# w_out of a hybrid SSD and attention layer as three products of split float32 parts, with a new order around it

## What is computed

```
for i in range(DEPTH):                       # DEPTH = 2
    x = x + 0.5 * swiglu(rms_norm(x, ffn1_norm[i]), ...)
    h = rms_norm(x, mix_norm[i])
    proj = h @ w_in[i]
    z, xbc, dt_raw, q, k, v = jnp.split(proj, splits, axis=-1)
    xbc = jax.nn.silu(causal_depthwise_conv(xbc, conv_w[i], conv_b[i]))
    y_ssd = ssd_mixer(xbc, dt_raw, z, ...)   # ends with y*silu(z) and a norm per group
    ...
    y_att = dilated_attention(q, k, v).reshape(b, s, ATT_WIDTH)
    x = x + jnp.concatenate([y_ssd, y_att], axis=-1) @ w_out[i]
    x = x + 0.5 * swiglu(rms_norm(x, ffn2_norm[i]), ...)
```

## Time and profile before

| | us |
|---|---|
| median of three runs | 2320.53 |
| lowest and highest of them | 2316.15, 2330.11 |
| the profiled execution's own time | 2322.31 |
| its span in the profile | 2320.5 |
| mean granted clock of PE over the span | 0.974 of full |

### The profile page before, as it was taken

One profiled execution on the slowest core, in us unless ns is written; L12 is line 12 of the kernel. 1 busy time (PEld: TensorE's weight loads), 2 busy tenths in 40 slices (PEclk: granted clock), 3 DMA queues, 4 the chain that ended last, 5 costly groups with the idle time before them and its releaser, 6 DMA issues.

```text
span 2320.5 us, 33951 instructions
## 1 busy us (share of the span) xinstructions
PE 2173.7 (94%) x12936; PEld 1850.1 (80%) x12936; DVE 1617.4 (70%) x2310; ACT 1058.2 (46%) x1267; POOL 446.3 (19%) x235
## 2 busy tenths in 40 slices
PE   5999999999999999899999989999889999999995
PEld 5998999569998998898579988988566777767774
DVE  5755869348558655878367553681389999999997
ACT  3333153334334341343234322212068888887874
POOL 8501644017007104372035000000000000000000
PEclk9999999999999999999999999999989999999998
DMA  8664655246656664464156643345458888888883
GB/s 247 223 194 146 208 156 190 73 136 227 208 174 209 207 198 159 153 201 141 55 200 200 207 145 109 111 126 198 164 198 335 345 341 342 342 339 332 335 343 130
DMA packets 241023, 484.25 MB, mean 209 GB/s; under 512 B 12660, under 2 KB 180880, under 8 KB 224560
## 3 DMA queue, kind: packets, MB, share of 16 engines
q1 hardware_dynamic: 226880, 443.58, 55.2%
q0 software_dynamic: 11424, 37.44, 4.8%
q10 hardware_dynamic: 2640, 2.14, 0.3%
HBM read 482.03 MB, written 1.09 MB: 208 GB/s over the span
## 4 chain that ended last, share of the span: by engine, by line
PE 70%; DVE 18%; ACT 7%; issue 3%; DMA 1%; DVEq 0%; ACTq 0%
PE misc L708 9%; PE misc L709 9%; PE misc L710 9%; PE misc L820 8%; DVE ring_low L2600 6%; PE acc L978 4%; PE acc L708 3%; ACT high_b L1754 3%; PE acc L710 3%; PE acc L709 3%; PE misc L1229 3%; PE misc L1231 2%; DVE arena L2097 2%; DVE ring_low L1981 2%; PE misc L1217 1%
## 5 line engine op out<-in xcount | busy, mean ns | idle before, releaser
L708 PE MATMUL misc<-xl,high_b 128*128 128x256 f32 x1408 | 395.8, 281 | 15.2 <-DVE ring_low L1981 15.2
L709 PE MATMUL misc<-xh,ring_low 128*128 128x256 f32 x1408 | 394.2, 280 | 0.0
L710 PE MATMUL misc<-xh,high_b 128*128 128x256 f32 x1408 | 393.9, 280 | 0.0
L2600 DVE TENSOR_TENSOR ring_low<-ring,high_b 128x2048 fp32r<-128x2048 f32 x128 | 287.0, 2284 | 6.8 <-ACT high_b L1754 6.8
L708 PEld LDWEIGHTS misc<-xl,high_b 128*128 128x128 f32 x1408 | 267.9, 190 | 19.6 <-issue 13.8
L709 PEld LDWEIGHTS misc<-xh,ring_low 128*128 128x128 f32 x1408 | 268.0, 190 | 3.3
L710 PEld LDWEIGHTS misc<-xh,high_b 128*128 128x128 f32 x1408 | 268.9, 191 | 0.0
L820 PE MATMUL misc<-xnT,ring 128*128 128x256 f32 x1152 | 253.2, 381 | 0.0
L820 PEld LDWEIGHTS misc<-xnT,ring 128*128 128x128 f32 x1152 | 219.1, 191 | 30.4 <-issue 0.8
L1981 DVE TENSOR_TENSOR ring_low<-ring,high_b 128x2048 fp32r<-128x2048 f32 x88 | 221.2, 2555 | 23.9 <-ACT high_b L1517 23.9
L1548 ACT ACTIVATE arena<-arena 128x256 f32<-128x256 f32 x88 | 36.8, 418 | 434.2 <-DVE arena L2015 434.2
(11 more groups left out here) (375 smaller groups left out, 4472.9 us busy)
## 6 DMA issues: line engine op xcount, KB each, us to landing
ring<-in_w_dram SPq DMA_DIRECT2D x128, 1024.0 KB, 7.0
ring<-in_w_in_dram SPq DMA_DIRECT2D x72, 1024.0 KB, 5.7
ring_d<-in_w_dram SPq DMA_DIRECT2D x128, 512.0 KB, 5.3
ring<-in_ffn_w_gate_dram SPq DMA_DIRECT2D x44, 1024.0 KB, 5.5
ring<-in_ffn_w_up_dram SPq DMA_DIRECT2D x44, 1024.0 KB, 7.9
ring_d<-in_ffn_w_down_dram SPq DMA_DIRECT2D x88, 512.0 KB, 7.5
arena<-in_w_ada_dram POOLq DMA_DIRECT2D x48, 512.0 KB, 5.0
ring<-in_w_out_dram SPq DMA_DIRECT2D x20, 1024.0 KB, 5.0
```

The costliest lines, as they stand in the source:

```text
L708: pe.matmul(dst, wh, ml, start=start, stop=False, **kw)
L709: pe.matmul(dst, wl, mh, start=False, stop=False, **kw)
L710: return pe.matmul(dst, wh, mh, start=False, stop=stop, **kw)
L2600: dve.tensor_tensor(ring_low[:, s, :], ring[:, s, :], high_b[:, s, :].bitcast(F32), ALU.subtract)\
```

## The change

- `out_rows` uses `three`: twelve fp32r matmuls in place of four float32 ones. ACT makes the high part of each of w_out's eight 1 MB blocks (`high_out`), DVE the low part (`low_out`). The high parts lie in three homes (`OUT_HOME`), each reused when its block has been read. The turned outputs are split too: ACT writes the high part (`y_high`), DVE the low part (`y_low`).
- The SSD's squares move from DVE to ACT (an ACTIVATE with Square behind `high_out(0)` and `high_out(1)`); DVE makes the first low part instead, and waits for the squares.
- Each group of `yt` and each turned group of heads is now drained by ACT and then DVE, not by one of them.
- `TURNS` comes one step later, `UNITS` has another order, and row 13 stands behind the last turn.
- SP waits for blocks 6 and 7 of w_out to be read before it loads the first rows of `w_down` of the second feed-forward layer.

```diff
-TURNS = {7: 0, 11: 1, 15: 2}
-UNITS = {0: 0, 1: 1, 2: 2, 3: 3, 4: 4, 7: 5, 8: 8, 9: 9, 11: 6, 12: 10, 13: 11, 15: 7, 16: 12, 18: 13}
+TURNS = {8: 0, 12: 1, 16: 2}
+UNITS = {0: 0, 1: 1, 2: 2, 3: 3, 4: 4, 6: 5, 9: 8, 10: 9, 11: 6, 12: 7, 13: 10, 15: 11, 17: 12}
+OUT_HOME = {0: 0, 1: 1, 2: 2, 3: 1, 4: 0, 5: 2, 6: 0, 7: 1}
+OUT_HIGHS = {1: 2, 5: 4, 7: 3, 9: 5, 12: 6, 15: 7}
+OUT_LOWS = {0: 1, 2: 2, 6: 4, 8: 3, 10: 5, 14: 6, 16: 7}
...
                     for q in range(2):
                         load_pair(n, i, q, w[0], w[1], c * P + q * BLK)
+                        if which and not q:
+                            for b in (6, 7):
+                                wait_slot_read(sp, RING["wout", l] + b)
                         for j in range(2 * q, 2 * q + 2):
...
                 def out_rows(k, halves=range(2)):
-                    n = n0 + k // 2
-                    if k >= KD:
-                        wait_drained(pe, m0 + AF["Y", (k - KD) // 2])
-                    wait_slot(n)
-                    w = rows_part(n)
+                    b = k // 2
+                    n = n0 + b
+                    wait_drained(pe, m0 + AF["Y", (k - KD) // 2] if k >= KD else FILL["yt", l] + k // 2)
+                    wait_split(pe, low_in, n)
+                    wh, wl = out_high_rows(b)[:, k % 2, :], out_low_rows(n)[:, k % 2, :]
...
-                            mm = pe.matmul(acc[:, t, c * 512:(c + 1) * 512], yT[:, k, t * P:(t + 1) * P],
-                                           w[:, k % 2, c * 512:(c + 1) * 512], start=(k == 0), stop=(k == 15),
-                                           skip_group_check=True)
+                            ts = slice(t * P, (t + 1) * P)
+                            mm = three(acc[:, t, cs], y_high(k)[:, ts], y_low(k)[:, ts], wh[:, cs], wl[:, cs],
+                                       k == 0, k == 15, skip_group_check=True)
...
                 turn_values(3)
+                out_rows(13).then_inc(freed[(n0 + 6) % SLOTS], 1)
                 out_rows(14, [0])
...
+            def high_out(l, b):
...
+                act.wait_ge(loaded[n % SLOTS], LOAD * (n // SLOTS + 1))
+                act.activation(out_high(b), ring[:, n % SLOTS, :], ACT.Copy).then_inc(high_in[n % SLOTS], 1)
...
+                for b in range(2):
+                    high_out(l, b)
+                act.wait_ge(yz_ready, l + 1)
+                act.activation(xdt.rearrange("p t e -> p (t e)"), xtok.rearrange("p t e -> p (t e)"), ACT.Square)\
+                    .then_inc(ysq_ready, 1)
                 act.wait_ge(sq_ready, 2 * l + 2)
                 act.activation(gss, gs, ACT.Sqrt).then_inc(std_ready2, 1)
...
+                for q in range(4):
+                    ssd_turned(q)
                 for h in range(HEADS + 2):
...
                     if h in TURNS:
                         values_turned(TURNS[h])
+                    if h in OUT_HIGHS:
+                        high_out(l, OUT_HIGHS[h])
...
-                link(dve.tensor_tensor(flat_dt, flat, flat, ALU.mult))
+                low_out(l, 0)
+                dve.wait_ge(ysq_ready, l + 1)
                 link(dve.tensor_reduce(gs, heads_of(flat_dt, 8), AX_X, ALU.add))
...
+                for q in range(4):
+                    ssd_low(q)
                 for h in range(HEADS + 3):
                     if h < HEADS:
                         maxima(h)
                     if 1 <= h <= HEADS:
                         weights(h - 1)
+                    if h in TURNS:
+                        values_low(TURNS[h])
                     if h >= 3:
                         attended(h - 3)
+                    if h in OUT_LOWS:
+                        low_out(l, OUT_LOWS[h])
+                values_low(3)
```

More of the change, by code:

```diff
@@ L493, in two_blocks @@
         SPLIT += [(RING["win", l] + 8, 16) for l in range(DEPTH)]
+        SPLIT += [(RING["wout", l], 8) for l in range(DEPTH)]
         def split_count(n):
@@ L575, in high_w_part, with out_high, out_high_rows, out_low_rows @@
             return high_w(b).rearrange("p (k f) -> p k f", k=KD)
+        def out_high(b):
+            if OUT_HOME[b] == 2:
+                return high_b[:, 0, :]
+            return ring_d_low[:, 2 * OUT_HOME[b]:2 * OUT_HOME[b] + 2, :].rearrange("p a b -> p (a b)")
+        def out_high_rows(b):
+            return out_high(b).rearrange("p (a f) -> p a f", a=2)
+        def out_low_rows(n):
+            return ring_low[:, n % SLOTS, :].rearrange("p (a f) -> p a f", a=2)
+        def y_high(k):
+            if k < KD:
+                return high_b[:, 1, k * SEQ:(k + 1) * SEQ]
+            return high_r[:, (k - KD) // 4, (k - KD) % 4 * SEQ:((k - KD) % 4 + 1) * SEQ]
+        def y_low(k):
+            return xh[:, k, :] if k < KD else xl[:, k - KD, :]
         def turned_qk(part_, k):
@@ L1570, in ffn @@
                 four(0, NF - 4, True)
+            def high_out(l, b):
+                n = RING["wout", l] + b
+                if b == 2:
+                    wait_filled(act, FILL["yt", l] + 3)
+                elif b < 2:
+                    wait_slot_read(act, RING["win", l] + 8 + (15, 13)[b])
+                else:
+                    wait_slot_read(act, RING["wout", l] + max(a for a in OUT_HOME if a < b and OUT_HOME[a] == OUT_HOME[b]))
+                act.wait_ge(loaded[n % SLOTS], LOAD * (n // SLOTS + 1))
+                act.activation(out_high(b), ring[:, n % SLOTS, :], ACT.Copy).then_inc(high_in[n % SLOTS], 1)
             def ssd_and_projections(l):
@@ L1658, in attention, with ssd_turned @@
                 scale = HD ** -0.5
+                def ssd_turned(q):
+                    m = FILL["yt", l] + q
+                    if q == 0:
+                        wait_filled(act, m + 3)
+                    for kk in range(2):
+                        k = 2 * q + kk
+                        ins = act.mul(y_high(k), bank_of(m)[:, kk * SEQ:(kk + 1) * SEQ],
+                                      cola[:, l, C_SSD + k:C_SSD + k + 1])
+                    ins.then_inc(yh_ready, 1)
                 def values_turned(q):
@@ L1662, in values_turned @@
                     wait_filled(act, m)
-                    act.activation(yT[:, KD + 2 * q:KD + 2 * q + 2, :], bank_of(m).rearrange("p (a b) -> p a b", a=2),
-                                   ACT.Copy).then_inc(drained[m % 4], 1)
+                    dst = high_r[:, q // 2, q % 2 * 512:(q % 2 + 1) * 512]
+                    act.activation(dst, bank_of(m), ACT.Copy).then_inc(yh_ready, 1)
+                for q in range(4):
+                    ssd_turned(q)
                 for h in range(HEADS + 2):
@@ L2273, in attended, with ssd_low, values_low @@
                         .then_inc(drained[m % 4], 1)
+                def ssd_low(q):
+                    m = FILL["yt", l] + q
+                    dve.wait_ge(yh_ready, 8 * l + q + 1)
+                    for kk in range(2):
+                        k = 2 * q + kk
+                        ins = dve.scalar_tensor_tensor(out=y_low(k), in0=bank_of(m)[:, kk * SEQ:(kk + 1) * SEQ],
+                                                       scalar=cola[:, l, C_SSD + k:C_SSD + k + 1],
+                                                       in1=y_high(k).bitcast(F32), op0=ALU.mult, op1=ALU.subtract)
+                    ins.then_inc(drained[m % 4], 1)
+                def values_low(q):
+                    m = m0 + AF["Y", q]
+                    dve.wait_ge(yh_ready, 8 * l + 4 + q + 1)
+                    for kk in range(2):
+                        k = KD + 2 * q + kk
+                        ins = dve.tensor_tensor(y_low(k), bank_of(m)[:, kk * SEQ:(kk + 1) * SEQ],
+                                                y_high(k).bitcast(F32), ALU.subtract)
+                    ins.then_inc(drained[m % 4], 1)
+                for q in range(4):
+                    ssd_low(q)
                 for h in range(HEADS + 3):
```

15 lines of the change are left out of this document (10 added, 5 removed).

## The result

The changed kernel takes 2325.58 us (median of 20 runs, 2317.08 to 2330.95), the kernel before 2318.09 us beside it (20 runs, one of them far off at 3584.18 us). The ratio is 1.0032, 95% interval 1.0022 to 1.0041: 7.4 us slower, and about 5 to 10 by the interval. The forecast was 2326, 5.6 us slower. A difference of 0.3% is small, but its interval leaves out 1. The profiled execution has a span of 2326.9 us and a mean granted clock of 0.970, against 2320.5 us and 0.974.

What follows compares the result with a forecast made beforehand. PE was taken to bound the attention stage, with DVE's SSD chain releasing it beforehand. Terms summed to +2.8 us per layer, +5.6 for two, giving 2326 us on the median of 2320.53; range 2309 to 2343.

Steps and rivals of the forecast that it cites:

- rows at full clock: w_out rows in the attention stage: three passes save 0.84 us per row, 15 rows, 12.6 us per layer.
- first row, with the clock's later return: First w_out row, at half clock: gains 1.3 us, while the later return of full clock costs 1.0 per layer.
- squares on ACT: End of the SSD branch, before the 16 transposes: squares behind two high parts delay it, costing 8.2 us per layer.
- scores of head 0: After the last SSD transpose: PE waits for the first bank's hand-over from ACT and DVE, 1.7 us per layer.
- first turn: Bare steps 7 and 8: new wait before the scores of head 9, released by DVE, 3.3 us per layer.
- clock behind it: After the first turn's wait: a half-clock stretch costs 1.7 us per layer; 5 if longer, 0 if none.
- tail: Turns in steps 12 and 16: waits at head 14's values, row 12 and last turn; net 1.4 us, bounds 0 and 3.3.
- slack before the add: Behind the stage, before the residual add: existing slack absorbs 0.6 us of PE's later end per layer.
- waits paid once: Rival: the turn's wait is hidden and the clock stays up; -4.6 us per layer, 2311 in all; chance 0.20.
- Half clock at every turn: Slower rival: each of three turns per layer brings 10.2 us at half clock; 2343 us; chance 0.09.
- feed-forward layer did not starve: Rival claimed starving: weight blocks queue after 509.6 and land late, 5 us per layer, 2336 us; chance 0.09.
- Square needed no table: Rival claimed Square needs its own table: two more 1.28 us loads per layer, 2331 us; counted within the forecast's 0.57.

Runs made afterwards that it cites:

- plain rows: Changed kernel with w_out's rows as four plain float32 matmuls of the high parts, low-part products left out; 2344.63 us, ratio 1.0112 to the kernel before.
- both: Changed kernel with squares on DVE, two high parts behind ACT's root, and head 5's output ahead of the turned heads' low parts; 2302.69 us, ratio 0.9917.
- output_first: Changed kernel, squares as changed, with DVE's output of head h-3 ahead of the turned heads' low parts; 2317.42 us, ratio 0.9987 to the kernel before.

## Why the prediction was right, term by term

Measured in the first layer's stage, per layer:

| term | predicted | measured | from |
|---|---|---|---|
| rows at full clock | -12.6 | -9.8 | 12 x (3.59 - 2.96) + 3 x (3.57 - 2.84) |
| first row, with the clock's later return | -0.3 | 0.0 | 435.21 - 429.86 = 5.35, like the 5.38 of the earlier trace rows |
| squares on ACT | +8.2 | +8.1 | 12.38 - 4.32 |
| scores of head 0 | +1.7 | +1.9 | 1.93 |
| first turn | +3.3 | +3.1 | 3.13 |
| clock behind it | +1.7 | +2.4 | step of head 9 7.30, such a step at full clock 4.87 |
| tail | +1.4 | +0.9 | 0.57 + 0.40 + 0.66 - 0.69 |
| slack before the add | -0.6 | -0.45 | the old idle 0.45 before the transposes of x is gone |
| sum | +2.8 | +6.2 | the stage grew by 6.5 |

The second layer's stage grew by only 4.9. There the scores of head 0 take 1106.60 - 1105.78 = 0.82 us (1.57 before) and the first row 1111.13 - 1106.60 = 4.53 (5.38 before), since the first 13.7 us of half clock had passed by the end of the transposes; these two make up the 1.6 us between the layers. The forecast was the same for both layers, and it let the full clock return 3.4 us after the first row began; it returned at 435.1, 5.2 us after, in the first layer.

Each wait stood where the forecast put it, with the releaser it named. The experiments remove them one at a time: the squares chain in two parts, 4.5 and 3.6 us; the 0.9 us of the high part within the wait at the turn; the first bank's drain.

One term was mis-sized: "0.84 us per row at the full clock". It set a row inside the stage, 3.59 us, against twelve matmuls in a dense stretch, 2.75 us. Inside the stage the three passes take 447.92 - 444.96 = 2.96 us: the first matmul and the last have 0.33 and 0.32 us each to the next start, where the others have 0.23. That makes 0.63 us per row. The run with plain rows agrees: 10.3 us for the sixteen rows where the forecast had 13.9, so 3.6 us per layer too much; the rival named for the experiments, that the rows give less than counted, was thus true in part, and DVE and ACT were too full only by their order.

That the sum came out near all the same is partly luck. The stages cost 11.5 us where I had 5.6. In the profiles the rest of the program gave 5.1 back, though I had written that nothing changes there; this is less than the 8 us by which the rest differs among the twelve kernels that share its code. What the profiles show is half clock that the kernel before had behind its stages and in the feed-forward layer, and that the changed one had less of:

```profile
514.60:517.90 3.30, 3.30 (x17) 3.30 (x18) 3.27 (x5) 1.57 (x3) 2.84 (x2) 0.52 0.67 262
702.40:712.50 10.10, 9.73 (x47) 9.73 (x47) 7.88 (x15) 5.79 (x11) 2.66 (x1) 0.51 0.19 75
```

(before, first layer), while the changed kernel keeps its full clock behind the stage up to 700 us:

```profile
518.00:700.00 182.00, 181.36 (x1339) 170.61 (x1338) 121.39 (x146) 72.65 (x78) 55.06 (x23) 1.00 0.67 219
```

It has a stretch of 3.4 us at 708 us itself, where the kernel before has 10. Whether the change caused this, or the phase in which its stages end, no run tells. The plain-row kernel had such stretches again, and "both", whose stages are the shorter ones, has one of 10 us at 693. That the one profile of the kernel before has the longest rest of all thirteen leaves the question open.

Of the rivals, "waits paid once" was wrong: they are there in both layers. "Half clock at every turn" was wrong for the second and third turn; only the first has it, 6.8 us and not 10.2 behind its wait of 3.1. The feed-forward layer did not starve: ACT takes up its second pair of blocks 530.13 - 517.62 = 12.5 us behind the stage's end, 13.8 before, and PE does not wait there for a weight block. Square needed no table. The estimate by the Trainium skill (ScalarE: Activation LUTs, section "What ACT_TABLE_LOAD costs") was 1.89 us for it; the trace says 1.97.

## What to carry to other kernels

A cheaper matmul is worth the difference measured where it stands, at its entry and exit too, not in a dense stretch. Work that makes operands (splits, squares) must not stand ahead of a short instruction that a serial chain waits for: the same work behind the root and behind `attended`, with the squares on DVE, turned +0.3% into -0.8%. Where two steps of a software pipeline follow each other without a filler, put a filler between them, ahead of the instruction that needs a freed buffer (row 5 in step 8 took away three waits), and judge a new order by the clock it leaves as much as by its waits.

## What was not expected of the hardware

The half-clock stretch at the start of the stage mostly grows with the waits ahead of it. Behind a wait of 4.3 us alone it was 10.2 or 10.3 us long, in all six stages that had it so (before, and the two kernels with a bank drained as it fills). With a second wait of 1.9 us behind the transposes it was 13.6 or 13.7 us, in nine stages of ten; behind waits of 7.9 and 1.9 it was 17, and behind 12.4 and 1.9 it was 20.5 us in six stages of eight. The exceptions had the same waits to the hundredth. The second layers of the changed kernel and of `output_first` had 13.7 us, full clock for 3.4, and 3.4 at half clock again. The first layer of "both" had only two stretches of some 3.3 us. So the waits alone do not settle it. The other stretch of the earlier trace rows, 3.3 us, which the prediction took as the short case, stands beside the longer wait of the two, 5.27 us:

```profile
296.30 1.11 PE L867 MATMUL misc<-konst,arena 128*128 128x128 f32 x4 [5.27 <-ACT arena L1595]
```

Behind the first turn, waits of 3.1, of 2.2, of 1.27 then 0.45, and of 0.45 then 1.13 us were followed by 6.7 to 6.9 us at half clock in the kernels with three passes, in both layers. The same wait of 3.1 with plain rows was followed by 3.4 us, in both layers. Waits of 0.45, 0.27 and 0.85 us were followed by none, in any of six stages (three kernels, two layers each). Waits that add up to the same can so differ by 3.4 us per layer. What decides it stays open.
